# Thirteen and ten unread identity products on TensorE, in the routing of a mixture-of-experts layer and ahead of its last sums

## What is computed

```python
def hier_moe(h, lw):
    g_logits = (h @ lw['moe_router_group_w'] + lw['moe_router_group_b']).astype(f32)
    _, grp = lax.top_k(g_logits, 1)
    e_logits = (h @ lw['moe_router_expert_w'] + lw['moe_router_expert_b']).astype(f32)
    ...
    top_v, top_i = lax.top_k(in_group, MOE_TOPK)
    w_top = jax.nn.softmax(top_v, -1) * jnp.take_along_axis(g_prob, grp, -1)
    ...
        hg = jnp.einsum('bld,edf->blef', h, lw['moe_w_gate'][e])
        hu = jnp.einsum('bld,edf->blef', h, lw['moe_w_up'][e])
        act = jax.nn.silu(hg) * hu * gate[..., e, None].astype(h.dtype)
        out = out + jnp.einsum('blef,efd->bld', act, lw['moe_w_down'][e])
```

## Time and profile before

| | |
|---|---|
| median of 3 runs | 1639.51 us (1638.74 to 1641.35) |
| profiled execution, its own time | 1640.04 us |
| its span, first to last instruction | 1638.2 us |
| mean granted TensorE clock | 0.976 |
| TensorE matmuls | 1523.8 us busy, 93% of the span |
| TensorE weight loads | 984.3 us, 60% (beside the matmuls) |
| VectorE | 741.3 us, 45% |
| ScalarE | 341.7 us, 21% |
| GpSimd | 205.6 us, 13% |

### The profile page before, as it was taken

How to read it: one execution, slowest core, us unless ns; L and a number is a source line. 1 busy time by engine, 2 the same in 40 slices (tenths; PEclk the granted TensorE clock), 3 DMA queues, 4 the chain that set the end, 5 groups by cost and what they waited for, 6 DMA issues and landing times.

```text
span 1638.2 us, 20753 instructions
## 1 busy us (share of the span) xinstructions
PE 1523.8 (93%) x8005; PEld 984.3 (60%) x8005; DVE 741.3 (45%) x1394; ACT 341.7 (21%) x633; POOL 205.6 (13%) x316
## 2 busy tenths in 40 slices
PE   8999999999999999999999999999999397978965
PEld 5888666577777777777777765666444232322312
DVE  5655199842534344636344323577844401101116
ACT  3001311412213131331313145000121211111113
POOL 3008300012111101101010010000000001101100
PEclk9999999999999999999999999999999699989997
DMA  7101011033221312111103120465200878675647
GB/s 218 52 26 52 18 40 35 30 121 102 64 71 52 111 42 73 49 56 52 48 35 125 48 106 32 174 274 180 110 39 26 292 262 327 245 263 207 224 171 301
DMA packets 47235, 194.70 MB, mean 119 GB/s; under 512 B 6408, under 2 KB 6904, under 8 KB 42400
## 3 DMA queue, kind: packets, MB, share of 16 engines
q1 hardware_dynamic: 28144, 116.13, 20.0%
q0 software_dynamic: 18992, 77.25, 13.2%
HBM read 353.23 MB, written 41.44 MB: 241 GB/s over the span
## 4 chain that ended last, share of the span: by engine, by line
PE 84%; DMA 6%; DVE 4%; issue 2%; SPq 2%; ACT 2%; POOL 0%; DVEq 0%; POOLq 0%; ACTq 0%
PE ps L548 29%; PE ps L616 7%; PE ps L896 7%; PE ps L945 6%; PE ps L1045 6%; PE ps L1059 3%; PE ps L840 3%; DMA arena<-in_w_gu 3%; PE ps L754 2%; PE ps L749 2%; PE ps L759 2%; PE ps L732 2%; SPq L475 1%; PE ps L563 1%; DMA scr<-h_rows,idx 1%
## 5 line engine op out<-in xcount | busy, mean ns | idle before, releaser
L548 PE MATMUL ps<-arena,wring 128*128 128x344 f32 x1728 | 528.5, 452 | 0.6 <-DVE arena L1471 0.6
L548 PEld LDWEIGHTS ps<-arena,wring 128*128 128x128 f32 x1728 | 314.4, 189 | 143.6 <-issue 1.9
L1045 PE MATMUL ps<-arena,scr 128*32 128x512 f32 x1280 | 150.4, 617 | 20.3 <-DMA arena<-in_w_gu 19.9
L2117 POOL DMA_DIRECT2D gate_scratch<-stage x96 | 52.1, 544 | 618.6 <-ACT stage L1185 542.8
L896 PE MATMUL ps<-arena,wring 128*128 128x344 f32 x384 | 111.2, 451 | 0.0
L1045 PEld LDWEIGHTS ps<-arena,scr 128*32 128x32 f32 x1280 | 39.3, 112 | 115.8 <-issue 83.7
L896 PEld LDWEIGHTS ps<-arena,wring 128*128 128x128 f32 x384 | 72.5, 189 | 38.6
L1185 ACT ACTIVATE stage<-ps 128x344 f32<-128x344 f32 x84 | 38.4, 457 | 252.8 <-PE ps L548 252.7
L2005 DVE TENSOR_TENSOR scr<-scr,ps 128x256 f32<-128x256 f32 x20 | 8.4, 421 | 181.4 <-ACT scr L1368 181.4
L1059 PE MATMUL ps<-arena,scr 128*32 128x512 f32 x640 | 76.1, 617 | 15.3 <-issue 13.9
L1702 DVE TENSOR_TENSOR scr<-scr,ps 128x512 f32<-128x512 f32 x40 | 27.5, 688 | 127.9 <-PE ps L754 127.9
(11 more groups left out here) (450 smaller groups left out, 2091.8 us busy)
## 6 DMA issues: line engine op xcount, KB each, us to landing
arena<-in_w_gu SPq DMA_DIRECT2D x336, 512.0 KB
arena<-in_w_dn SPq DMA_DIRECT2D x80, 1024.0 KB
wring<-in_w_all SPq DMA_DIRECT2D x55, 512.0 KB, 3.6
gate_scratch<-stage POOLq DMA_DIRECT2D x96, 172.0 KB, 2.2
arena<-gate_scratch POOLq DMA_DIRECT2D x4, 2064.0 KB, 10.5
scr<-gate_scratch POOLq DMA_DIRECT2D x4, 2064.0 KB, 10.4
arena<-y_rows SPq DMA_DIRECT2D x16, 512.0 KB, 9.6
arena<-in_w_out SPq DMA_DIRECT2D x2, 2048.0 KB, 15.7
```

The costliest lines, as they stand in the source:

```text
L548: mm = pe.matmul(ps[:, c, 0:CW], wring[:, slot, k, :], H[:, k, chunk(c)], start=k == 0, stop=k == KT - 1)
L1045: mm = pe.matmul(ps[S * j:S * (j + 1), i % 2, :], XT[i % 2][:, k * P + S * j:k * P + S * (j + 1)], GU[j][:, k * 2 * HID:(k + 1) * 2 * HID] ...
L2117: pool.dma_start(gate_scratch[:, g:g + 1, chunk(c)], stage[:, c:c + 1, :]).then_inc(sem(f"gate_out{c}"), 16)
```

## The change

`idle_products(k)` issues k products of the 128x128 identity (stationary) with the first 512 columns of the constants (moving) into PSUM bank 0, with no wait and no semaphore. Nothing reads them. It is called four times in TensorE's program: 5 before the wait for the membership table, 5 before the wait for the scatter tables, 3 before the first gathered rows, and 10 between the last step's `down` and the last sums. No other engine's program is changed.

```diff
+            def idle_products(k):
+
+                for _ in range(k):
+                    pe.matmul(ps[:, 0, :], ident, cst[:, 0:HALF], start=True, stop=True)
+
+            idle_products(5)
             pe.wait_ge(sem("routed"), 1)
             for b, m in ((4, tri), (5, ones)):
...
             pe.matmul(ps[0:1, 7, 0:NSLOTS], ECOL, ident[:, 0:NSLOTS], start=True, stop=True).then_inc(sem("slot_mm"), 1)
 
+            idle_products(5)
             for a in range(V18):
                 if a % NTT == 0:
                     pe.wait_ge(sem("routed"), 4 + a // NTT)
...
+            idle_products(3)
             turn_rows(0)
             turn_rows(1)
             gate_up(0)
...
                     gate_up(i + 1)
                 down(i)
 
+            idle_products(10)
             pe.wait_ge(sem("diag"), 2 * len(ON_PE))
```

## The result

| | before | after |
|---|---|---|
| median of 9 runs | 1641.01 us (1636.74 to 1643.55) | 1647.42 us (1641.78 to 1650.87) |
| ratio to before | | 1.0037, 95% interval 1.0023 to 1.0052 |
| profiled execution, its own time | 1640.04 us | 1644.05 us |
| its span | 1638.2 us | 1642.2 us |

The kernel became slower by some 6 us. That is outside the range of the forecast, 1636.3 to 1642.2. Two later series of the same kernel gave 1.0037 (1.0025 to 1.0049) and 1.0033 (1.0017 to 1.0050).

What follows compares the result with a forecast made beforehand. In the routing VectorE sets the pace, then a gather and a weight transfer; at the end, rows read back and VectorE. -0.3 - 0.4 - 0.1 = -0.8 us gives 1639.2, as median 1638.7; range 1636.3 to 1642.2.

Steps and rivals of the forecast that it cites:

- Price of a product: One added product on TensorE, two instructions, costs 0.85 us at full clock and 1.70 at half.
- First five: Routing, ahead of the membership table: products end 2.0 us early at full clock, hidden by VectorE; gain -0.3 us.
- slow rival: Routing: products don't hold the clock and delay the work, 1.0 us, then 2.0 more; 1642.5 to 1644.3, chance 0.06.
- Second five: Routing, ahead of L1010: 6.0 us, half clock first, ending 0.5 us early; L1010 gains -0.4 us, L1014 -0.1.
- Three: Ahead of the first gathered rows: hidden by the gather even when slow; nothing else queued behind any product; cost nothing.
- First expert step: Transposes and 16 instructions some 2.6 us shorter, weight wait over 4 us, next 48 instructions open by 1.75 either way: 0.
- Ten at the end: Ahead of the last sums: end at 1598.1, clock may fall again, VectorE's 2.83 us wait for out_y covers it: 0.
- The sum: Whole kernel: -0.3 - 0.4 - 0.1 = -0.8 us, from the profiled 1640.04 to 1639.2.
- range: Whole kernel: 1636.3 to 1642.2, from under the full-clock first step to the low end of the slow case.
- share of 0.06 for slower: Whole kernel slower by over 0.2%: chance 0.06, made of 0.04 from the slow case and 0.02 for the unexplained.
- rule on throttled time: Routing, first step and end: a held clock gives back 23.9 us by the skill's rule; rival at 1615.6, chance 0.01.

Runs made afterwards that it cites:

- first_five: Kernel before plus only the five full-size products ahead of the wait for the membership table: ratio to before 1.0017 (1.0000 to 1.0034).
- routing_only: Kernel before plus only the 5, 5 and 3 products in the routing, none ahead of the last sums: ratio to before 1.0020 (1.0002 to 1.0037).
- change_pad_256: The whole change plus 51 one-element products in the routing, a shift of 256 instructions, run in two series: ratios to before 0.9997 and 1.0005.
- end_only: Kernel before plus only the 10 products ahead of the last sums: ratio to before 1.0002 (0.9987 to 1.0017).

## Why the prediction was wrong, point by point

- **Price of a product**: right. Ten instructions at full clock took 4.54 us by the timeline, 4.3 were said.
- **First five**: right in the trace of the change, with the clock up and TensorE free 2 us early; VectorE's wait for L1006 fell from 0.33 to 0.23 us, so the gain was 0.1, not 0.3. The first five depend on the execution: where the clock was low when they began (`first_five`, `routing_only`, both change_pad_256) L1000 came 0.65 to 1.6 us late. This is the half of the slow rival that I had put at 1.0 us. It happens, but it is not what costs 6 us.
- **Second five**: half clock first, then full, as described; 6.92 us with 6.0 said, and 0.2 us in the way instead of 0.5 us early. VectorE's wait fell from 1.10 to 0.69, a gain of 0.4 as taken.
- **Three**: right, hidden by the gather. The gathered rows are turned 0.44, 0.64 and 0.52 us sooner in the three traces of the change, for 0.8 said.
- **First expert step**: the number, 0, was right (it ends at 41.91, 41.93 and 41.77 us for 41.96), the way to it was not. The clock was to be up, the transposes and the 16 instructions some 2.6 us shorter in sum (by the halves that the prediction names it would be 3.0) and the wait for the weights over 4 us. In the change the clock had fallen again (0.78 and 0.71 in these stretches), the three took 1.63, 1.94 and 2.99 us for 1.97, 1.94 and 2.83, the wait was 2.42 us and the 48 took 7.05 us as before. That nothing changed here is luck as far as the mechanism goes.
- **Ten at the end**: right at 0; `end_only` is 1.0002. The clock fell again before the sums had got far (0.83 over the stretch 1600 to 1610), as feared.
- **The step that failed** stands under "Three": "Nothing else is queued behind any of the products on TensorE, no semaphore is added, and no DMA queue, SP's or POOL's, sees an instruction more." It is true word for word and leaves out the queue through which TensorE's own program comes (q8 above). The 13 products move TensorE's program by 52 instructions against its fetch blocks of 256, and a fetch of about 0.9 us moved into the last load of expert weights, on the path. The prediction put the expert stage behind its first step at nothing; the runs show +5.5 us there. Of these, about +1.1 us are the load with the fetch in it and 3.75 are steps 17 and 18 in all; how the shift makes the rest is open.
- **The sum**, -0.8 us, is neither shown nor refuted: with 128 or 256 instructions of shift in place of 52 the change has 1.0007, 0.9997 and 1.0005, and the interval of each holds both -0.8 us and 0.
- The **range** left the shift out entirely. Every rival was about the work and the clock of the products; none moved the program without them. The share of 0.06 for slower was too small because the only slow case was one whose conditions looked unlikely, while a kernel that waits for its loads in eight steps may be slowed in any of them.
- The **rule on throttled time** did not come true. The Trainium skill (TensorE: Matmul & The Clock Gate, Terms) would make the kernel faster by the clock given back. From 1280 to 1310 the granted clock rose by 0.43, 0.23 and 0.26, which by that rule is some 9 us, as an estimate, and the first gathered rows were turned 0.44 us sooner; the change with a shift of 128, where the clock was up at the first five too, was not faster.

## What to carry to other kernels

In this kernel 13 one-element products in TensorE's program, ahead of loads that it later waits for, cost some 4 us without doing anything, and 64 of them cost nothing: they move the fetches of its program against the loads. Before a small loss or gain is put down to what an edit does, time a null version of it, with the same number of instructions in the same place and next to no work, and one padded to a whole block of 256. And where a trace is late ahead of the edit, count from a common point and compare more than one trace.

## What the runs showed that was not expected

- With a 16 KB instruction fetch 6.5 to 7.4 us into it, the load of the down weights was about 1.1 us longer, near the 0.9 us for which the fetch held one DMA engine, and only its last two large packets were clearly late. The Trainium skill (Runtime: NRT & Kernel Launch, Instruction fetch mechanics) calls the cost mostly hidden. These runs agree for most of the expert stage, in which the steps that wait for no load take 11.68 us in nearly every trace; they don't agree for a fetch inside that load, which TensorE waits for.
- A delay of 1 us is not the end of it: the idle time of TensorE grew from some 2.4 to some 3.5 us, and the matmuls behind it took 4.94 to 6.54 us in all seven builds with the long wait, where they take 3.64 at full clock. Behind the short wait they took 5.05 us or more in seven builds of twelve.
- The execution time of one kernel scatters with a standard deviation of 2.2 to 3.3 us in series of 22 or more runs of before, so that 3 runs do not show 0.2%, and a single trace can be 3 us off by chance.
